# Second projection of the first MLP: half its blocks in three rounded products, kernel copies on ScalarE, another place for the near fetch

## What is computed

```python
x = x + gate_f * (jnp.square(jax.nn.relu(h @ w_fc1[layer])) @ w_fc2[layer])   # layer 0: 1024 -> 4096 -> 1024
...
h = _rmsnorm(x, norm_g[layer, 0]) * (1.0 + scale_m) + shift_m                # layer 1 begins
mix = _mixer_s5(h, ...)      # a state space model, 64 groups of 16 channels
```

## Time and profile before

| what | value |
| --- | --- |
| median of three runs | 1170.21 us (1169.49 to 1174.09) |
| the profiled execution, its own time | 1172.47 us |
| its span in the profile | 1170.6 us |
| granted TensorE clock, mean over the span | 0.982 |
| TensorE busy | 1113.4 us, 95% |
| VectorE busy | 829.1 us, 71% |
| ScalarE busy | 558.1 us, 48% |

### The profile page before, as it was taken

The page is one execution under the profiler, slowest core; times in us unless marked ns, Lnnn a source line. Parts: engine busy times, 40 slices in busy tenths (PEclk is TensorE's granted clock), DMA queues, the critical chain, the costliest instruction groups (busy, mean ns, idle before and its releaser), DMA issues.

```text
span 1170.6 us, 21137 instructions
## 1 busy us (share of the span) xinstructions
PE 1113.4 (95%) x8970; PEld 971.9 (83%) x8970; DVE 829.1 (71%) x1414; ACT 558.1 (48%) x876; POOL 45.0 (4%) x71
## 2 busy tenths in 40 slices
PE   7899898999999997879999999999989999999998
PEld 4788676988888885469988888899978899988898
DVE  1699466877578674875677764578898966659955
ACT  3224633445101124653555543456677846467944
POOL 0010011000000000000000000000000000042000
PEclk9999998999999998999999999989999999999999
DMA  9977688899848957865455555525432345343342
GB/s 374 377 279 270 229 327 305 306 333 329 342 181 251 346 191 157 329 246 180 144 180 184 187 194 190 180 80 173 158 130 78 133 151 180 130 152 117 107 145 72
DMA packets 38287, 246.41 MB, mean 210 GB/s; under 512 B 4400, under 2 KB 5584, under 8 KB 9648
## 3 DMA queue, kind: packets, MB, share of 16 engines
q1 hardware_dynamic: 29072, 182.36, 45.8%
q0 software_dynamic: 6240, 43.94, 9.9%
q10 hardware_dynamic: 2880, 18.74, 3.9%
HBM read 225.24 MB, written 19.79 MB: 209 GB/s over the span
## 4 chain that ended last, share of the span: by engine, by line
PE 78%; DVE 10%; DMA 5%; ACT 4%; issue 2%; SPq 0%; ACTq 0%; DVEq 0%
PE ps L1494 11%; PE ps L1498 10%; PE ps L1496 10%; PE ps L1520 10%; PE ps L1501 10%; PE ps L1521 5%; PE ps L1645 4%; DMA ca_dram<-more 2%; PE ps L1738 1%; DMA more<-in_ada_w 1%; PE ps L2182 1%; PE ps L1593 1%; DVE ada_more L2974 1%; PE ps L1691 1%; PE ps L1871 1%
## 5 line engine op out<-in xcount | busy, mean ns | idle before, releaser
L1494 PE MATMUL ps<-rounded_parts,w_high_rounded 128*128 128x256 f32 x1136 | 328.9, 290 | 2.2 <-DVE rounded_parts L2335 1.3
L2328 DVE TENSOR_TENSOR ring_rounded<-ring,w_high_rounded 128x1024 fp32r<-128x1024 f32 x220 | 260.8, 1227 | 88.9 <-ACT w_high_rounded L882 88.5
L1496 PE MATMUL ps<-rounded_parts,w_high_rounded 128*128 128x256 f32 x1136 | 322.9, 284 | 0.0
L1498 PE MATMUL ps<-rounded_parts,ring_rounded 128*128 128x256 f32 x1136 | 322.8, 284 | 0.0
L882 ACT ACTIVATE w_high_rounded<-ring 128x1024 fp32r<-128x1024 f32 x220 | 219.8, 1049 | 63.8 <-PE ps L1521 48.2
L1494 PEld LDWEIGHTS ps<-rounded_parts,w_high_rounded 128*128 128x128 f32 x1136 | 219.6, 193 | 11.4 <-issue 6.7
L1496 PEld LDWEIGHTS ps<-rounded_parts,w_high_rounded 128*128 128x128 f32 x1136 | 219.6, 193 | 0.2
L1498 PEld LDWEIGHTS ps<-rounded_parts,ring_rounded 128*128 128x128 f32 x1136 | 219.4, 193 | 0.0
L1520 PE MATMUL ps<-rounded_parts,w_high_rounded 128*128 128x512 f32 x496 | 175.3, 399 | 0.0
L1521 PE MATMUL ps<-rounded_parts,ring_rounded 128*128 128x256 f32 x496 | 139.3, 281 | 0.0
L1501 PE MATMUL ps<-big,ring 128*128 128x256 f32 x544 | 121.0, 381 | 0.0
(11 more groups left out here) (426 smaller groups left out, 1555.1 us busy)
## 6 DMA issues: line engine op xcount, KB each, us to landing
ring<-in_blocks SPq DMA_DIRECT2D x139, 1024.0 KB, 4.9
ada_w<-in_ada_w POOLq DMA_DIRECT2D x27, 1024.0 KB, 7.5
ada_more<-in_ada_w POOLq DMA_DIRECT2D x13, 1024.0 KB, 7.5
we_dram<-we_t ACTq DMA_DIRECT2D x8, 1024.0 KB, 7.8
ca_dram<-more ACTq DMA_DIRECT2D x8, 1024.0 KB, 10.8
ring<-we_dram SPq DMA_DIRECT2D x8, 1024.0 KB, 5.7
ring<-ca_dram SPq DMA_DIRECT2D x8, 1024.0 KB, 7.2
big<-in_ada_w SPq DMA_DIRECT2D x4, 1024.0 KB, 11.3
```

What stands on the lines that cost most here:

```text
L1494: nc.tensor.matmul(out, high[:, k, columns], x_high, start=start, stop=False, skip_group_check=True)
L1496: nc.tensor.matmul(out, high[:, k, columns], x_low, start=False, stop=False, skip_group_check=True)
L1498: last = nc.tensor.matmul(out, low[:, k, columns], x_high, start=False, stop=stop, skip_group_check=True)
L2328: nc.vector.tensor_tensor(rounded(w), w, w_high[:, c % 2, ks], ALU.subtract)\
```

## The change

Blocks 4 to 11 of `fc2_0`, in a new order (the table `FC2_0`), are done in three rounded products. They are the blocks with k = 2 and 3, for all n. The first four and the last four blocks stay plain. ScalarE rounds the activations of these two row blocks in eight pieces of 128x512 (`round_deep`) and VectorE subtracts them (`lower_deep`). Each of the eight weight blocks is rounded and lowered in two halves as in `fc1_0`. The kernels of each slice are copied out of PSUM by ScalarE (`copy_kernels`), and VectorE keeps the diagonal. The tables of places for the slices are new, and so are the lists of ScalarE and VectorE. The exponential is taken ahead of the angles. The near pieces 0 and 1 are fetched together ahead of the last block of `fc2_0`, pieces 2 and 3 behind the first and second block of the mixer's `we`, into the part of `big` that blocks 4 to 11 have read.

```diff
...
-S5_TURN_AT = (7, 11, 15, 18, 20, 22, 24, 26)
-S5_KERNEL_AT = (9, 13, 17, 19, 21, 23, 25, 27)
+S5_TURN_AT = (7, 11, 14, 16, 19, 22, 24, 27)
+S5_KERNEL_AT = (9, 13, 15, 18, 21, 24, 26, 28)
+FC2_0 = [(0, 0), (0, 1), (0, 2), (1, 0), (2, 0), (3, 0), (2, 1), (3, 1), (2, 2), (3, 2), (2, 3), (3, 3), (1, 1), (1, 2),
+         (0, 3), (1, 3)]
+FC2_0_SPLIT = range(4, 12)
+FC2_0_FIRST = [[n for _, n in FC2_0].index(n) for n in range(4)]
+FC2_0_LAST = [max(j for j, (_, m) in enumerate(FC2_0) if m == n) for n in range(4)]
...
-    phase("fc2_0", [("fc2_0", k, n) for n in range(4) for k in range(4)])
+    phase("fc2_0", [("fc2_0", k, n) for k, n in FC2_0])
...
-            if b - start not in {"w_in": W_IN_SPLIT, "w_out": W_OUT_SPLIT}.get(name, range(end - start)):
+            if b - start not in {"w_in": W_IN_SPLIT, "w_out": W_OUT_SPLIT, "fc2_0": FC2_0_SPLIT}.get(name, range(end - start)):
...
-    NEAR_AT = (first_block["fc2_0"] + 10, first_block["fc2_0"] + 11)
+    NEAR_AT = first_block["fc2_0"] + FC2_0_SPLIT.stop + RING - 1
...
-                             big[:, 2048:4096], big[:, 4096:6144])]
+                             big[:, 4096:6144], big[:, 6144:8192])]
...
+        deep_high = (sq, hT)
...
+        for n in range(4):
+            ready[first_unit["fc2_0"] + n] = first_block["fc2_0"] + FC2_0_LAST[n] + 1
...
-                if b in NEAR_AT:
-                    load_near(NEAR_AT.index(b))
+                if b == NEAR_AT:
+                    load_near(0)
+                    load_near(1)
...
-                    if nb == RING - 1:
-                        load_near(2)
-                        load_near(3)
+                    if nb < 2:
+                        load_near(2 + nb)
...
+            def copy_kernels(m):
+                act.wait_ge(kext_psum, m + 1)
+                if m > 0 and m % 2 == 0:
+                    act.wait_ge(k_stored, 16 * (m // 2))
+                edge, lane = (L - 1) * GC, 2 * (m % 2)
+                dst = kext[:, :, lane:lane + 2].rearrange("p x a -> p a x")
+                nc.scalar.activation(dst[:, :, 0:edge],
+                                     STAT[:, 0:2 * P].rearrange("p (a x) -> p a x", a=2)[:, :, 0:edge], ACT.Copy)
+                nc.scalar.activation(dst[:, :, edge:WIN], MISC[2][:, 0:2 * P].rearrange("p (a x) -> p a x", a=2),
+                                     ACT.Copy).then_inc(kext_copied, 1)
...
                 if n in (8, 12):
                     store_outputs(n // 4 - 2)
-                if n == 11:
-                    store_kernels(0)
-            store_kernels(1)
+                if n == 14:
+                    store_kernels(1)
+                if n < 15 and n in S5_KERNEL_AT:
+                    copy_kernels(S5_KERNEL_AT.index(n))
             store_outputs(2)
-            for m in range(3, 8):
-                if m == 3:
-                    modulation_row(ADA_PIECES - 1)
-                if m == 4:
-                    modulation_row(ADA_PIECES)
+            def round_deep(pairs):
+                for q in pairs:
+                    act.wait_ge(hid_ready, 8 + q + 1)
+                    act.wait_ge(blocks_done, first_block["fc2_0"])
+                    round_tiles(deep_high[q // 4][:, 2 * (q % 4):2 * (q % 4) + 2], hid[:, 16 + 2 * q:16 + 2 * q + 2])
+            def turned_weights(m):
                 copy_weights(m, (0, 1, 2, 3))
                 store_weights(m)
-                store_kernels(m - 1)
-                store_outputs(m)
+            deep = first_block["fc2_0"]
+            round_deep(range(4))
+            copy_kernels(2)
+            round_deep(range(4, 8))
+            turned_weights(3)
+            round_to(deep + 5)
+            store_outputs(3)
+            modulation_row(ADA_PIECES - 1)
+            copy_kernels(3)
+            round_to(deep + 6)
+            modulation_row(ADA_PIECES)
+            turned_weights(4)
+            store_kernels(3)
+            store_outputs(4)
+            round_to(deep + 7)
+            copy_kernels(4)
+            round_to(deep + 8)
+            turned_weights(5)
+            round_to(deep + 9)
+            store_outputs(5)
+            round_to(deep + 10)
+            turned_weights(6)
+            copy_kernels(5)
+            round_to(deep + 11)
+            store_kernels(5)
+            round_to(deep + 12)
+            store_outputs(6)
+            copy_kernels(6)
+            turned_weights(7)
+            nc.scalar.activation(shrink[:, :, 1:NCH], s5_a.unsqueeze(2).to_broadcast([P, GROUPS, NCH - 1]), ACT.Exp,
+                                 scale=float(L))
+            store_outputs(7)
+            copy_kernels(7)
             store_kernels(7)
             act.wait_ge(k_stored, 16 * 4)
             act.wait_ge(rot_args, 1)
-            nc.scalar.activation(shrink[:, :, 1:NCH], s5_a.unsqueeze(2).to_broadcast([P, GROUPS, NCH - 1]), ACT.Exp,
-                                 scale=float(L))
             nc.scalar.activation(rot_sin, rot_cos, ACT.Sin)
             nc.scalar.activation(rot_cos, rot_cos, ACT.Sin, scale=0.5).then_inc(rot_fun, 1)
+            act.wait_ge(blocks_done, deep + FC2_0_SPLIT.stop)
             norm_stats(2, 2)
             shift(2, 1, SHIFT_M)
...
                 if m > 0:
-                    pe.wait_ge(kext_ready, m)
+                    pe.wait_ge(kext_copied, m)
                 edge = (L - 1) * GC
...
+            def deep_block(j):
+                kb, n = FC2_0[j]
+                ps = pair(start_unit("fc2_0", n) if j == FC2_0_FIRST[n] else bank_of(first_unit["fc2_0"] + n))
+                deep_low = split_arrived("fc2_0", 2)
+                def arrived(k):
+                    if j in FC2_0_SPLIT:
+                        deep_low(KB * (kb - 2) + k)
+                    elif k % 2 == 0:
+                        pe.wait_ge(hid_ready, (KB * kb + k) // 2 + 1)
+                def tile(k):
+                    if j in FC2_0_SPLIT:
+                        return rounded(deep_high[kb - 2][:, k]), rounded(hid[:, KB * kb + k])
+                    return hid[:, KB * kb + k]
+                block_products("fc2_0", j, arrived if n == 0 else None,
+                               [(k, ps[:, i], slice(P * i, P * i + P), tile(k),
+                                 j == FC2_0_FIRST[n] and k == 0 and i == 0, j == FC2_0_LAST[n] and k == KB - 1)
+                                for k in range(KB) for i in range(2)])
+                after_block(j)
+            for j in range(len(FC2_0)):
+                deep_block(j)
...
             def s5_kernels(m):
-                dve.wait_ge(kext_psum, m + 1)
+                dve.wait_ge(kext_copied, m + 1)
                 if m == 0:
                     dve.wait_ge(dq_here, 16)
-                elif m % 2 == 0:
-                    dve.wait_ge(k_stored, 16 * (m // 2))
                 edge = (L - 1) * GC
                 lane = 2 * (m % 2)
-                out = kext[:, :, lane:lane + 2].rearrange("p x a -> p a x")
-                nc.vector.tensor_copy(out[:, :, 0:edge], STAT[:, 0:2 * P].rearrange("p (a x) -> p a x", a=2)[:, :, 0:edge])
-                link(nc.vector.tensor_copy(out[:, :, edge:WIN], MISC[2][:, 0:2 * P].rearrange("p (a x) -> p a x", a=2)))
                 for a in range(2):
                     d = s5_dq[:, 2 * m + a:2 * m + a + 1]
...
             def s5_outputs(m, between=None):
                 if m > 0:
-                    s5_kernels(m - 1)
                     dve.wait_ge(ca_stored, 16 * m)
...
             s5_power_tables(lower_next)
             s5_inputs_scaled(lower_next)
             lower_next()
-            for m in range(2):
-                s5_weights(m, lower_next)
-                lower_next()
-                s5_outputs(m, lower_next)
-                lower_next()
+            s5_weights(0, lower_next)
+            lower_next()
+            s5_outputs(0, lower_next)
+            lower_next()
+            s5_weights(1, lower_next)
+            lower_next()
+            s5_kernels(0)
+            s5_outputs(1, lower_next)
+            lower_next()
             s5_weights(2, lower_next)
             lower_next()
             modulation(3)
+            s5_kernels(1)
             s5_outputs(2)
             gate_f = lambda k: mod(0, GATE_F, k)
-            for m in range(3, 8):
-                s5_weights(m)
-                s5_outputs(m)
-                if m in (4, 6):
-                    residual("fc2_0", gate_f, m // 2 - 2, m // 2 - 1)
-            residual("fc2_0", gate_f, 2, 3)
+            def lower_deep(pairs):
+                for q in pairs:
+                    lower_tiles("fc2_0", q, hid[:, 16 + 2 * q:16 + 2 * q + 2],
+                                deep_high[q // 4][:, 2 * (q % 4):2 * (q % 4) + 2])
+            s5_weights(3)
+            lower_deep(range(4))
+            s5_kernels(2)
+            s5_outputs(3)
+            lower_deep(range(4, 8))
+            s5_weights(4)
+            lower_next()
+            s5_kernels(3)
+            s5_outputs(4, lower_next)
```

(14 more changed lines are left out.)

18 lines of the change are left out of this document (3 added, 15 removed).

## The result

| what | before | after |
| --- | --- | --- |
| median | 1169.87 us (20 runs, 1167.28 to 1176.76 and one of 1563.7) | 1175.05 us (20 runs, 1168.81 to 1178.14) |
| ratio of after to before, 95% interval | | 1.003 (1.0016 to 1.0044) |
| the profiled execution, its own time; span | 1172.47; 1170.6 | 1176.61; 1174.8 |
| granted TensorE clock | 0.982 | 0.975 |

The change costs 0.3%: within the 0.5% that the prediction called no change, on the slow side of it, and inside the range. Against the forecast median of 1172.3 the measured 1175.05 is 2.75 us late. The profiled execution is 4.14 us longer than that of before, where 2.1 were forecast.

The account below looks back on a forecast made before the run. TensorE was taken to bound `fc2_0`, with VectorE nearly full after the change. Slices 9.2 later, tail 2.1 less, low clock 2 more, near fetch 7.0 less gave 2.1 us more: 1172.3 against the median, range 1161 to 1180.

Parts of the forecast that it names:

- part 1: Products of `fc2_0`: eight rounded blocks at 5.94 for 6.97 us save TensorE 8.2; VectorE's busy time rises from 100.8 to 117.8.
- Part 2: From the kernels of slice 3 to those of slice 7 in `fc2_0`: kernels 7 start 9.2 us later.
- The three waits: Ahead of slice 6's weights, VectorE waits for ScalarE's roundings of blocks 6, 7 and 8: 1.8, 2.2 and 2.1 us.
- Part 3: Kernels 7 to the norm: 27.6 us, 2.1 less; TensorE idles 5.3 us before the norm, low clock adds 2.
- Part 4: Mixer chunks behind the norm: earlier near pieces no longer hold up TensorE's instructions, stall and low clock go, 7.0 us less.
- The sum: Whole kernel: 9.2 - 2.1 + 2 - 7.0 = 2.1 us more than the profiled 1172.47.
- Rival 1: Slices of `fc2_0`: VectorE keeps up without the three waits, TensorE doesn't idle before slice 6; 1164 us, chance 0.20.
- Rival 2: Mixer chunk: TensorE's 5.71 us stall stays, the 7 us don't come back; 1179.3 us, chance 0.20.
- Rival 3: Slice stores take 14.8 us and the clock is low wherever TensorE idles; 1180 us, chance 0.08.
- Rival 4: Rounded blocks of `fc2_0` are no faster, 6.97 us each; time stays 1172, inside the main forecast, no chance of its own.

Follow-up runs that it names:

- a_four: Changed kernel with slices' places drawn in and only four blocks (k = 3) rounded, every second one from 5 to 11; 1166.43 us, 0.9941 of before.
- a_thin_lower: Changed kernel with VectorE lowering only 16 of 256 columns of each of the eight weight blocks, TensorE's work and all waits kept; 1167.59 us, 0.9971 of before.
- b_shift20: Kernel before with 20 short products added at TensorE's start, moving its later instructions by 40 records; 1172.54 us, ratio 1.0013.
- b_near_late: Kernel before with near pieces 2 and 3 issued behind the eighth `we` block, not the fourth; 1169.4 us, ratio 1.0000.
- b_early_near: Kernel before with the change's block order, all blocks plain, and its new places of near pieces 2 and 3; 1165.61 us, ratio 0.994.
- a_near_back: Changed kernel with near pieces 2 and 3 back behind the fourth `we` block; 1175.19 us, 1.0048 of before.
- the two shifts: Kernel before with TensorE's instruction stream moved by 40 or by 80 records through short products at its start; ratios 1.0013 and 1.0054.
- a_four_res: a_four with the residual of column block 1 moved on VectorE from ahead of the diagonal of kernels 7 to behind the angles; 1160.72 us, 0.9907 of before.

## Why the prediction was right

**What bounds the kernel, part 1.** Right. The rounded block was taken at 5.94 and measured at 5.86 (in a_four); a lowered piece of activations at 0.6, measured 2.49 for four; two halves of a block at 2.3, measured 2.36. VectorE was put at 117.8 us; up to the norm it has 113.1. ScalarE's two copies were taken at 0.8 and last 1.06 (393.28 to 394.34). The gain of 8.2 us came through in no kernel with eight such blocks.

**Part 2, the race.** Right, and this carried the forecast. The three waits were put at 1.8, 2.2 and 2.1, and came as 1.72, 1.99 and 2.25; the idle time ahead of slice 6 at 6.4, and came as 6.93. The work behind it took 393.2 - 387.49 = 5.7 in place of 3.65, so the 2 us for the clock were right. Kernels 3 to 7: forecast 88.3, measured 87.4. What it had wrong is the last leg, from outputs 6 to kernels 7. The sum has the store there, 10.9 us, and then outputs 7. The store of outputs 6, issued at 407.39, had landed by 414.96 at the latest (no wait there), within 7.6 us, and VectorE made the weights of slice 7 in the meantime: the store is not on the path. Kernels 7 start 16.7 us behind kernels 6 and wait for nobody. TensorE's own work in between is 1.38 + 5.94 + 2.27 + 6.97 = 16.6. The forecast 10.9 + 7.28 = 18.2 was near it by luck. a_thin_lower bears out that VectorE's work is part of the cause: 6.1 of the 87.4 us.

**Part 3, the tail.** Right: 27.6 forecast, 27.8 measured, with TensorE idle 5.43 (5.3). The clock was put at 2 us; norm to chunk 0 takes 15.96 against 13.32 before, so 2.6 (1.5 to 2.6 in the kernels with this idle time).

**Part 4, the near fetch.** Right in size: 7.0 forecast, and chunk 0 to near takes 6.7 us less. The reading of the stall as TensorE's instructions, held up by the near pieces, is borne out by b_shift20, where the stop moved by 39 records for 40 put in, by b_near_late, and by the packets. b_early_near shows that in the kernel before the early place is worth 6.4 us. But the reason given for the changed kernel did not hold, and here the forecast had luck. The pieces were to end 18 to 26 us behind kernels 7 and before 450. Their last issue ends at 440.3, but the queue stays full, with a share of 1.06 from 450 to 455 and 0.56 from 455 to 460: by the landings in the trace the last piece is there at 455.4, 31 us behind kernels 7. The stall is absent because TensorE comes late, by the idle time and the low clock of part 3, and a_near_back, with the pieces in their old place, has none either. So the 7.0 us are not the worth of the new place in this kernel; they are the worth of coming late, in part paid for by part 3. (Chunk 0 also has 32 records, 9 + 23, and not the 16 that the text of part 4 says.)

The Trainium skill, Runtime: NRT & Kernel Launch, section Instruction fetch mechanics, says that a crossing costs one bump of a DMA queue, mostly hidden. For most crossings the trace agrees, as TensorE shows no such stop elsewhere in this stage; where the near pieces, or the `we` blocks behind them, load the queue it differs, with 5.71, 7.72, 2.12, 1.88 and 1.80 us, and there the measurements decide. The section also gives a page as 256 instructions. Each record of TensorE has one of its weight load beside it (x9098 of each), so a page would be 128 records by an estimate; the 126 of the two shifts and of the 71 packets are near it.

**The sum.** Forecast 9.2 - 2.1 + 2 - 7.0 = 2.1; the read of the near pieces comes at 492.05 against 487.78, 4.3 later. Of that 1.65 us are there before the stage's first block (310.19, where 307.16 + 1.38 = 308.54 was counted), in a part that the change doesn't touch: TensorE reaches the first blocks of `w_in` from the ring at 45.25 against 43.35, and no run shows why. The other 2.6 are the change. In parts: kernels 7 come 8.6 us later (9.2), the tail takes 1.9 less (2.1), norm to chunk 0 takes 2.6 more (2), chunk 0 to near 6.7 less (7.0). The medians differ by 5.2 us, and the ratio's interval allows 1.9 to 5.1.

**The rivals.** Rival 1 (VectorE keeps up) fell: 1164 was reached by no version with eight rounded blocks. Rival 2 (the stall stays) fell by its effect, not by its condition: the pieces did land more than 28 us behind kernels 7. Its deciding point, a last near issue more than 18 us behind kernels 7, was too simple as well: there are 1.8 to 1.9 us of stall at 22.0 and 23.4, but none at 19.6 (b_early_near) and none at 30.5 (a_near_back). What decides is whether the queue is still full when TensorE passes the cut before. In the five kernels that stop, the packet starts 4.2 to 9.1 us behind that; in the nine others, within 1.9. Rival 3 (stores drag) fell by the store that landed within 7.6 us. Rival 4 fell too, by the 5.86 us.

## What to carry to other kernels

A stage that is bound by one engine with a second one nearly full gains from a cheaper instruction only as far as the second follows: lay the second engine's list beside the first, with its waits, and choose how many pieces to convert (here four of sixteen gained, and eight, with other places, did not). After an edit of the order, look at every step that waits for a block and stands in front of the chain that ends the stage: one residual in the wrong place cost 5.3 us and the clock behind it. And a transfer that nobody waits for can still stop an engine; move it to where the queue is free, not only away from the stall. A stall that is gone after an edit may only be hidden by another delay: put the edit back alone, as a_near_back does, before you book the gain.

## What the runs showed of the hardware

- TensorE stops for its own instructions when the queues are full as it passes the cut before, here for 1.8 to 7.7 us, with "issue" as the releaser. The packet on the instruction queue then starts 4.2 to 9.1 us after that cut, else within 1.9 us.
- The cuts lie about 126 records apart (8970 records, 71 packets). The place of the stop moves with the number of instructions ahead of it, so an edit far away, even 20 short products at the start, can move such a stop; an edit that changes when TensorE arrives can bring or remove it.
- After 5 to 7 us of idle time TensorE ran at 0.50 of its clock (1.2 of 2.4 GHz): 16 records of a turned slice took 3.77 us, 2.27 on the full clock; the norm's 12 records took 5.46, in a_four_res 2.92. On the path that was 2.0 us ahead of slice 6, and 1.5 to 2.6 us ahead of the norm over the kernels with such a gap there.
